# Splitting two weight pieces with one operation, and the last strip block by block, in a two-layer encoder on one core

## The reference

```python
h = x
# layer 0: pooling mixer, then MLP
h = h + multiscale_pool_mixer(rms_norm(h, mix_norm[0]), pool_w[0], pool_scale[0])
h = h + sqrelu_mlp(rms_norm(h, mlp_norm[0]), w_mlp_in[0], w_mlp_out[0])
k, v = shared_kv(h, kv_norm, w_kv, cos, sin)          # 2048 -> 4096, partial rotary on K
# layer 1: differential attention (8 heads, chunk mask), then MLP
h = h + diff_attention(rms_norm(h, mix_norm[1]), k, v, w_q[0], lam[0], subln[0], w_o[0], cos, sin, 1)
h = h + sqrelu_mlp(rms_norm(h, mlp_norm[1]), w_mlp_in[1], w_mlp_out[1])
return rms_norm(h, final_norm)

def sqrelu_mlp(h, w_in, w_out):                        # 2048 -> 8192 -> 2048
    u = jax.nn.relu(h @ w_in)
    return (u * u) @ w_out
```

## Time and profile before

| what | value |
|---|---|
| median of three runs | 1880.54 us (1879.68 to 1880.59) |
| time of the profiled execution | 1880.07 us |
| its span in the profile | 1878.1 us |
| TensorE busy (matmuls) | 1848.9 us, 98% of the span, 8425 matmuls |
| VectorE busy | 1145.9 us, 61% |
| ScalarE busy | 837.6 us, 45% |
| mean DMA rate | 185 GB/s |

### The profile page before, as it was taken

The page is one execution under the profiler, slowest core; times in us unless marked ns, Lnnn a source line. Parts: engine busy times, 40 slices in busy tenths (PEclk is TensorE's granted clock), DMA queues, the critical chain, the costliest instruction groups (busy, mean ns, idle before and its releaser), DMA issues.

```text
span 1878.1 us, 24422 instructions
## 1 busy us (share of the span) xinstructions
PE 1848.9 (98%) x8425; PEld 1536.9 (82%) x8425; DVE 1145.9 (61%) x1404; ACT 837.6 (45%) x1057; POOL 10.6 (1%) x14
## 2 busy tenths in 40 slices
PE   7999999999999999999999999999999999999997
PEld 6888888888888888888888878888888888888886
DVE  7656665656566556755557776556555655556665
ACT  6544444444444444643444545444444444444442
POOL 0000000000000000000000000000000000000000
PEclk9999999999999999999999999999999999999998
DMA  7655566556565655566554456565556565555552
GB/s 275 191 190 179 184 196 190 190 187 192 185 194 183 197 190 182 167 200 191 190 185 157 135 160 201 178 193 187 192 192 194 189 191 184 189 187 179 189 192 89
DMA packets 178441, 348.17 MB, mean 185 GB/s; under 512 B 10642, under 2 KB 10852, under 8 KB 178148
## 3 DMA queue, kind: packets, MB, share of 16 engines
q1 hardware_dynamic: 177696, 345.74, 57.5%
q10 hardware_dynamic: 708, 1.94, 0.3%
HBM read 345.55 MB, written 2.10 MB: 185 GB/s over the span
## 4 chain that ended last, share of the span: by engine, by line
PE 58%; issue 38%; DVE 3%; ACT 1%; DMA 0%; POOL 0%; SPq 0%; POOLq 0%; DVEq 0%; ACTq 0%
PE bank L916 18%; PE bank L914 18%; PE bank L915 18%; PE bank L932 2%; DVE w_lo L590 1%; DMA h<-in_x 0%; DVE h L636 0%; DVE a_lo L614 0%; PE bank L1052 0%; PE bank L998 0%; DVE b_lo L608 0%; PE bank L1000 0%; PE bank L1068 0%; ACT probs L532 0%; ACT scratch L381 0%
## 5 line engine op out<-in xcount | busy, mean ns | idle before, releaser
L372 ACT ACTIVATE w_hi<-raw 128x1024 fp32r<-128x1024 f32 x640 | 669.5, 1061 | 806.3 <-PE bank L916 801.3
L590 DVE TENSOR_TENSOR w_lo<-raw,w_hi 128x1024 fp32r<-128x1024 f32 x640 | 764.6, 1220 | 308.2 <-ACT w_hi L372 304.1
L914 PE MATMUL bank<-w_hi,a_hi 128*128 128x512 f32 x1344 | 527.6, 393 | 0.0
L916 PE MATMUL bank<-w_hi,a_lo 128*128 128x512 f32 x1344 | 523.3, 389 | 0.0
L915 PE MATMUL bank<-w_lo,a_hi 128*128 128x512 f32 x1344 | 523.1, 389 | 0.0
L914 PE MATMUL bank<-w_hi,b_hi 128*128 128x512 f32 x1248 | 488.2, 391 | 0.0
L916 PE MATMUL bank<-w_hi,b_lo 128*128 128x512 f32 x1248 | 485.8, 389 | 0.0
L915 PE MATMUL bank<-w_lo,b_hi 128*128 128x512 f32 x1248 | 485.6, 389 | 0.0
L636 DVE TENSOR_TENSOR h<-bank,h 128x512 f32<-128x512 f32 x288 | 185.4, 686 | 230.5 <-PE bank L916 230.5
L916 PEld LDWEIGHTS bank<-w_hi,a_lo 128*128 128x128 f32 x1344 | 252.3, 188 | 52.6
L915 PEld LDWEIGHTS bank<-w_lo,a_hi 128*128 128x128 f32 x1344 | 252.5, 188 | 50.9
(11 more groups left out here) (82 smaller groups left out, 358.4 us busy)
## 6 DMA issues: line engine op xcount, KB each, us to landing
raw<-in_w_mlp_in SPq DMA_DIRECT2D x256, 512.0 KB, 3.8
raw<-in_w_mlp_out SPq DMA_DIRECT2D x256, 512.0 KB, 4.8
raw<-in_w_kv SPq DMA_DIRECT2D x64, 512.0 KB, 4.2
raw<-in_w_q SPq DMA_DIRECT2D x32, 512.0 KB, 4.8
raw<-in_w_o SPq DMA_DIRECT2D x32, 512.0 KB, 4.2
raw<-in_pool_w SPq DMA_DIRECT2D x8, 512.0 KB, 7.7
h<-in_x SPq DMA_DIRECT2D x4, 512.0 KB, 6.5
out<-scratch SPq DMA_DIRECT2D x3, 512.0 KB, 4.6
```

Of the source, the lines that this page charges most:

```text
L372: nc.scalar.activation(w_hi[:, n], raw[:, n % RAW], ACT.Copy).then_inc(hi_ready, 1)
L590: nc.vector.tensor_tensor(w_lo[:, n], raw[:, n % RAW], w_hi[:, n].bitcast(F32), ALU.subtract).then_inc(lo_ready, 1)
L914: nc.tensor.matmul(banks[tb][:], hi[:, tok], w_hi[:, n, kk, :], start=begin, stop=False)
L916: last = nc.tensor.matmul(banks[tb][:], lo[:, tok], w_hi[:, n, kk, :], start=False, stop=end)
```

## The change

Two things are done.

**Pairs.** From the second strip on, ScalarE makes w_hi of both pieces of a group in one operation of 2 x 1024 columns, and VectorE makes w_lo of both in one. ScalarE's operation waits for both pieces to have landed and for TensorE to have finished both pieces of that group in the strip before. `hi_ready` and `lo_ready` go up by two. Loads are still single, 512 KB each.

**The last strip.** It no longer goes group by group over both token halves, but block by block: first the four groups of the first token half, then the four of the second, each block (tb, g) of 12 matmuls in a bank of its own (`LAST`, all eight banks). VectorE adds each block to h and multiplies it with the final gain, and ScalarE takes its squares. The norm of the first half is finished and its rows scaled (one operation of 2048 columns) and stored (one store) while TensorE works on the second half. The second half is scaled in pieces of 640, 640 (VectorE) and 768 columns (ScalarE).

```diff
-DVE_PIECES = [(0, slice(0, D // 2)), (0, slice(D // 2, D)), (1, slice(D // 2, D))]
-ACT_PIECES = [(1, slice(0, D // 2))]
+DVE_PIECES = [(0, slice(0, D)), (1, slice(0, 640)), (1, slice(640, 1280))]
+ACT_PIECES = [(1, slice(1280, D))]
...
+        LAST = (psum[2:6], psum[0:2] + psum[6:8])
...
             def split(s, g, first=False):
 
-                for n in (2 * g, 2 * g + 1):
-                    act.wait_ge(raw_landed[n % RAW], 16 * (2 * s + n // RAW + 1))
-                    if not first:
-
-                        act.wait_ge(pe_done, (s - 1) * HALVES + n + 1)
-                    nc.scalar.activation(w_hi[:, n], raw[:, n % RAW], ACT.Copy).then_inc(hi_ready, 1)
+                at = 2 * g % RAW
+                for i in range(2):
+                    act.wait_ge(raw_landed[at + i], 16 * (2 * s + 2 * g // RAW + 1))
+                if not first:
+
+                    act.wait_ge(pe_done, (s - 1) * HALVES + 2 * g + 2)
+                nc.scalar.activation(w_hi[:, 2 * g:2 * g + 2], raw[:, at:at + 2], ACT.Copy).then_inc(hi_ready, 2)
...
             def split(s, g):
 
-                for n in (2 * g, 2 * g + 1):
-                    dve.wait_ge(hi_ready, s * HALVES + n + 1)
-                    nc.vector.tensor_tensor(w_lo[:, n], raw[:, n % RAW], w_hi[:, n].bitcast(F32), ALU.subtract).then_inc(lo_ready, 1)
+                at = 2 * g % RAW
+                dve.wait_ge(hi_ready, s * HALVES + 2 * g + 2)
+                nc.vector.tensor_tensor(w_lo[:, 2 * g:2 * g + 2], raw[:, at:at + 2], w_hi[:, 2 * g:2 * g + 2].bitcast(F32),
+                                        ALU.subtract).then_inc(lo_ready, 2)
...
+            for tb in range(TB):
+                for g in range(NG):
+                    cols = slice(g * SW, (g + 1) * SW)
+                    dve.wait_ge(pe_done, (STRIPS - 1) * HALVES + tb * NG + g + 1)
+                    nc.vector.tensor_tensor(h[:, tb, cols], LAST[tb][g][:], h[:, tb, cols], ALU.add).then_inc(last_added, 1)
+                    dve.wait_ge(last_added, tb * NG + g + 1)
+                    nc.vector.tensor_tensor(result[:, tb, cols], h[:, tb, cols], final_row[:, cols], ALU.mult).then_inc(gained, 1)
+                    if tb == 1 and g == 0:
+                        last_norm(0)
+                    if tb == 1 and g == 1:
+                        last_scale(0, *DVE_PIECES[0])
+            last_norm(1)
+            for i in (1, 2):
+                last_scale(i, *DVE_PIECES[i])
...
+            def last_strip(s, at, done):
+
+                pe.wait_ge(t_taken, (NJ - 1 + R_U[1]) * 2 + 2)
+                for tb in range(TB):
+                    tok = slice(tb * P, (tb + 1) * P)
+                    for g in range(NG):
+                        if tb == 0:
+                            pe.wait_ge(h_added, done - 1 if g < 2 else done)
+                        for hf in range(2):
+                            n = 2 * g + hf
+                            pe.wait_ge(lo_ready, s * HALVES + n + 1)
+                            for kk in range(2):
+                                hi, lo = b_tile(at + 2 * hf + kk)
+                                edge = 2 * hf + kk
+                                nc.tensor.matmul(LAST[tb][g][:], hi[:, tok], w_hi[:, n, kk, :], start=edge == 0, stop=False)
+                                nc.tensor.matmul(LAST[tb][g][:], hi[:, tok], w_lo[:, n, kk, :], start=False, stop=False)
+                                last = nc.tensor.matmul(LAST[tb][g][:], lo[:, tok], w_hi[:, n, kk, :], start=False, stop=edge == 3)
+                        last.then_inc(pe_done, 1)
```

More of the change, by code:

```diff
@@ L267, in trunk @@
         o_done = sem("o_done")
+        last_added = sem("last_added")
+        last_squared = sem("last_squared")
         gained = sem("gained")
@@ L358, in _ @@
                 nc.gpsimd.tensor_tensor(o_rms[:, t, :], o_mean[:, t, :], neg_half[:], ALU.pow).then_inc(o_rms_done, 1)
-            for k in range(3, 5):
-                inv_rms(k)
+            inv_rms(3)
+            for tb in range(TB):
+                pool.wait_ge(mean_done, 5 + tb)
+                nc.gpsimd.tensor_tensor(rms[:, 4, tb:tb + 1], mean[:, 4, tb:tb + 1], neg_half[:, 0:1], ALU.pow).then_inc(rms_done, 1)
         @block.scalar
@@ L446, in mlp @@
                         u_hi(NJ - 1, layer, U_LAST)
-                for g in range(NG):
-                    if layer == 0:
+                if layer == 0:
+                    for g in range(NG):
                         split(s0 + 2 * NJ, g)
-                    h_squares(k + 2, g, H_MLP[layer] + NG * (NJ - 1) + g + 1)
-                    if layer == 0 and g >= 2:
-                        h_hi(1, g - 2)
+                        h_squares(k + 2, g, H_MLP[layer] + NG * (NJ - 1) + g + 1)
+                        if g >= 2:
+                            h_hi(1, g - 2)
+                else:
+                    for tb in range(TB):
+                        for g in range(NG):
+                            act.wait_ge(last_added, tb * NG + g + 1)
+                            if tb or g:
+                                act.wait_ge(last_squared, tb * NG + g)
+                            nc.scalar.activation(junk[:, g % 2], h[:, tb, g * SW:(g + 1) * SW], ACT.Square,
+                                                 accum_out=ssq[:, 4, tb, g:g + 1]).then_inc(last_squared, 1)
             act.dma_start(keep[:, 0:P], keep_consts[:, 0:P]).then_inc(ident_landed, 16)
@@ L573, in _ @@
             mlp(1)
-            act.wait_ge(rms_done, 5)
-            act.wait_ge(gained, NG)
+            act.wait_ge(rms_done, 6)
+            act.wait_ge(gained, TB * NG)
             for i, (tb, cols) in enumerate(ACT_PIECES):
@@ L669, in mlp @@
                         u_lo(NJ - 1, layer, U_LAST)
[L670 to L680, removed]
+                if layer == 0:
+                    for g in range(NG):
+                        h_add(s0 + 2 * NJ - 1, g)
                         split(s0 + 2 * NJ, g)
@@ L889, in _, with last_norm, last_scale @@
             mlp(1)
[L892 to L895, removed]
-                nc.vector.tensor_scalar(result[:, tb, cols], result[:, tb, cols], rms[:, 4, tb:tb + 1], None, ALU.mult).then_inc(result_dve, 1)
+            def last_norm(tb):
+                dve.wait_ge(last_squared, NG * (tb + 1))
+                nc.vector.tensor_reduce(ssum[:, 4, tb:tb + 1], ssq[:, 4, tb, :], AX.X, ALU.add).then_inc(sum_done, 1)
+                dve.wait_ge(sum_done, 4 + tb + 1)
+                nc.vector.tensor_scalar(mean[:, 4, tb:tb + 1], ssum[:, 4, tb:tb + 1], 1.0 / D, EPS, ALU.mult, ALU.add).then_inc(mean_done, 1)
+            def last_scale(i, tb, cols):
+                dve.wait_ge(rms_done, 5 + tb)
+                dve.wait_ge(gained, NG * (tb + 1))
+                nc.vector.tensor_scalar(result[:, tb, cols], result[:, tb, cols], rms[:, 4, tb:tb + 1], None, ALU.mult).then_inc(result_dve, 1)
+            dve.wait_ge(final_landed, 16)
+            for tb in range(TB):
+                for g in range(NG):
+                    cols = slice(g * SW, (g + 1) * SW)
[10 more added lines that the diff above has]
+                last_scale(i, *DVE_PIECES[i])
         @block.tensor
@@ L978, in mlp @@
                 done = h0 + NG * (NJ - 1)
-                out_strip(s0 + 2 * NJ - 1, U_LAST, layer, NJ - 1,
-                          lambda g: turn_h(1, g - 2, done + g - 1) if g >= 2 and layer == 0 else None)
+                if layer == 0:
+                    out_strip(s0 + 2 * NJ - 1, U_LAST, layer, NJ - 1,
+                              lambda g: turn_h(1, g - 2, done + g - 1) if g >= 2 else None)
+                else:
+                    last_strip(s0 + 2 * NJ - 1, U_LAST, done)
             pe.wait_ge(ident_landed, 16)
```

## The result

The changed kernel takes 1889.23 us, median of five runs (1887.73 to 1889.6), against 1880.54 in the same sessions: a ratio of 1.0045, with a 95% interval of 1.0033 to 1.0056. It is slower by 8.7 us, in the direction forecast and inside the range, by more than the forecast 5.5. The profiled execution has a span of 1887.7 us, 9.6 more than before.

What follows compares the result with a forecast made beforehand. TensorE, busy 98% of the span, was taken as the bound. Attention +5.6, end of layer 0 +2.0, last strip -4.0 and clock +2.0 made +5.6, say 5.5 us: 1886.0 from 1880.54, range 1879.5 to 1889.5.

Steps and rivals of the forecast that it cites:

- Steady strips, 0: In the steady strips a pair takes longer from release to w_lo, but TensorE needs it 16.3 us later: cost 0.
- One sign that the prediction had set against itself: The prediction was to be wrong if, among other signs, ScalarE waits for raw in steady strips.
- the forecast 9.7 of 10.9 us: In steady strips a piece's release and reload take about 9.7 us, against a next use at 10.9.
- End of layer 0, +2.0: Last strip of layer 0 delayed 0.57 us, K strip stalled 1.41: together +2.0 us, bounds 0.6 and 2.4.
- The last strip, -4.0: At the tail the first store is issued 1.4 us earlier and 2.6 us of stores go: -4.0, bounds -3.0 and -4.5.
- Attention, +5.6: At t = 2 to 4 pairs delay o_n, for which TensorE's transposes wait: stalls 1.77, 2.31 and 1.48 us, together +5.6.
- Its upper bound of 6.8: Attention stalls with the upper prices of a pair (2.1 and 2.35), two of each in every t: 6.8 us.
- released at 4.2 to 4.5 us, landed 4.8 us later: Steady-strip load timing after a pair; with some 0.4 for the second issue, landing comes at about 9.7 us.
- ScalarE's slack behind a late landing is over 10 us: In steady strips, a late load leaves ScalarE over 10 us of slack, so the cost was taken as 0.
- The clock, +2.0 for one fall: TensorE's gaps of 1.8, 2.3 and 3.2 us bring one fall to half clock: +2.0 us, bounds 0 and 6.0.
- clock falls at two or three gaps: 1888 to 1890: Rival: TensorE's clock falls at two or three gaps, giving 1888 to 1890 us; chance of several falls 0.12.
- the likeliest case: Stalls with one clock fall, 1885 to 1888 us, chance 0.38.

Runs made afterwards that it cites:

- VectorE single: The changed kernel, but during the attention steps VectorE makes w_lo piece by piece behind ScalarE's pair: 1890.27 us, ratio 1.0049.
- the pairs alone: The kernel before with the two paired splits of the change and its old last strip: 1892.09 us, ratio 1.0062.

## Why the prediction was right, and where its sizes were off

**Steady strips, 0.** Right: with pairs there only, 1876.26 against 1876.23 without any. The reason given was right too: the release to w_lo takes longer and nobody waits. One sign that the prediction had set against itself did come: ScalarE waits for raw pieces in steady strips, nine times in the MLPs of the changed kernel (17.9 and 13.2 us) and 25 times in the run with pairs there only. So some loads land after TensorE has left the piece, which the forecast 9.7 of 10.9 us leaves no room for. The sign was badly chosen, since none of these waits reaches TensorE.

**End of layer 0, +2.0.** Right: 1.9 us by experiment. The new wait in the K strip is 1.17 idle plus 0.16, forecast 1.41, and it stands where it was put, at 784.

**The last strip, -4.0.** Right: 4.0 in the trace, 4.2 in the run with it alone, and the shape as well: one add and one square less, first store at 1883.21, 3.1 us after the last matmul's add began, half the bytes behind it.

**Attention, +5.6.** The mechanism was right and shown twice: it vanishes with single splits and with maxima ahead of the pair. The size was too small. Step by step, from the lateness of the transposes of line 1068 (the earlier trace rows against 1032.67, 1064.88 and 1098.99): 5.88, 8.37 and 11.90 us. Before any of that, TensorE's transposes of the keys at t = 1 start at 973.61 and not at 971.84, so 1.77 us of the lateness are older than the attention steps' pairs. Another 0.35 comes with the transposes of Q, which now wait for rope: they start at 999.27 and before at 997.21, and those of t = 2 are 2.12 late; forecast 0. So t = 2 cost 5.88 - 2.12 = 3.8, forecast 1.8; t = 3 cost 8.37 - 5.88 = 2.5, forecast 2.3 (the second maxima, at 1052.31 and before at 1043.89, came 2.5 later than TensorE's own lateness); t = 4 cost 11.90 - 8.37 = 3.5, of which 1.7 are the clock fall behind 1064.88, so 1.8, forecast 1.5. Together 8.4 in this profile. In the others t = 2 costs 2.3 or 2.4, so the pairs cost 0.35 + 2.3 + 2.5 + 1.9 = 7.0 us as a rule, 1.4 more than forecast. Part of it shows as TensorE's waits for maxima, which the prediction does not name. (Its upper bound of 6.8 is too low by its own prices: two operations on each engine in three steps, 0.18 and 0.07 dearer each, give 1.5 more than 5.6, so 7.1.)

The largest miss in one step is t = 2, and the table says what it left out: the pair's own 1.9 was forecast as 1.8, and the piece that lands late was taken as 0. The step that failed there is "released at 4.2 to 4.5 us, landed 4.8 us later": true in a steady strip, but around the end of t = 1 the pair of group 3 is split behind maxima, differences and rope, so its slots come free later. "ScalarE's slack behind a late landing is over 10 us" holds for TensorE's need, not for the maxima that stand behind that very split. That costs 0.4 to 0.7 in four profiles. Why the piece took 6.16 us to land in the first profile and 4.7 to 4.8 in three others with the same four loads stays open; the four loads alone do not make it so late.

**The clock, +2.0 for one fall.** The mechanism was right, the count wrong: two falls in the first profile, three in the second, one in the run with VectorE single (1098 to 1100 at 0.50) and one with the pairs alone. A fall costs 1.7 us, forecast 2.0. The rule of the Trainium skill (TensorE: Matmul & The Clock Gate, Why this matters for your kernels) that gaps between bursts cost the clock agrees with this; its practical limit would have let the gaps of 2.05 and 2.06 pass, and two profiles show falls behind such gaps. The tail's row had said so the earlier trace rows.

The sum by the measured terms, for the first profile: 1.8 up to t = 1 (the 2.1 of layer 0's end, and a start that was 0.35 earlier), 8.4 in the attention steps, 2 x 1.7 = 3.4 for the clock, and -4.0 in the last strip: 9.6, the difference of the two spans; the medians differ by 8.7.

**How near the sum came.** The direction held, but the measured 8.7 lies 3.2 above the forecast 5.5, and 1889.23 is only 0.3 below the range's upper end. It came out in the rival "clock falls at two or three gaps: 1888 to 1890", which had 0.12 of the chance and not the 0.38 of the likeliest case. No two errors offset each other: the attention term and the clock term were both too small.

## What to carry to other kernels

One operation over two pieces starts when the later piece is free, so before merging, ask for each place in the list who stands behind the operation, not how much fixed cost it saves: here 0.07 us per pair was on offer and some 2 us at each of a few steps were lost. Where a chain of small dependent steps runs between large ones on an in-order engine, put the small step ahead. Here a stall of 2.05 us on TensorE cost nearly twice itself, as 1.7 us more went through its clock.

## What the runs showed that was not expected

- Gaps of the same length are not treated alike. Behind 2.05 to 2.07 us the granted clock fell in three of four cases over the two profiles of the changed kernel, and not at all in the run with pairs and the old last strip (2.03 and 2.06); a gap of 2.56 passed once with the clock full, while unfilled gaps of 2.90 to 2.99 cost it in four of four profiles. Each fall costs 1.7 us. That it also makes the runs of one kernel differ by 2 to 3 us is likely and not shown by traces: with VectorE single, 1887.61 and 1888.02 had a mean granted clock of 0.998, and 1890.27, 1890.39 and 1890.59 one of 0.996 or 0.997.
- An idle time shown before a matmul is 0.16 us less than the time lost, as the trace ends the one before 0.39 after its start and the next would have started at 0.227.
